# Wide matmuls over both halves of an activation in a first up projection, and a gate's column sum in the down projection

## The reference

```python
mod = c_act @ w_ada[l] + b_ada[l]
sh1, sc1, g1, sh2, sc2, g2 = [m[:, None, :] for m in jnp.split(mod, 6, axis=-1)]
...
h = rmsnorm(x, norm_gains[l, 2]) * (1.0 + sc2) + sh2
y = jnp.square(jax.nn.relu(h @ w1[l] + b1[l])) @ w2[l] + b2[l]
x = x + g2 * rmsnorm(y, norm_gains[l, 3])
```

## Time and profile before

| | us |
|---|---|
| median of three runs | 787.77 |
| the profiled execution | 789.94 |
| its span from first to last instruction | 788.2 |
| PE busy | 734.8 (93% of the span) |
| VectorE busy | 517.8 (66%) |
| ScalarE busy | 450.2 (57%) |
| GpSimd busy | 44.4 (6%) |
| one low half `wl` on VectorE, mean of 217 | 1.23 |

### The profile page before, as it was taken

How to read it: one execution, slowest core, us unless ns; L and a number is a source line. 1 busy time by engine, 2 the same in 40 slices (tenths; PEclk the granted TensorE clock), 3 DMA queues, 4 the chain that set the end, 5 groups by cost and what they waited for, 6 DMA issues and landing times.

```text
span 788.2 us, 12072 instructions
## 1 busy us (share of the span) xinstructions
PE 734.8 (93%) x4062; PEld 619.8 (79%) x4062; DVE 517.8 (66%) x764; ACT 450.2 (57%) x724; POOL 44.4 (6%) x77
## 2 busy tenths in 40 slices
PE   0599999789999999989999999999897999999998
PEld 0498966589999886767989777777686888888886
DVE  6877697777877643457657465665747777777443
ACT  1654678666666433355455687554446777777331
POOL 3100100100000100014101000000000000000000
PEclk9899999979999999998999999999997999999999
DMA  8999985257787655534763564544444666656661
GB/s 315 368 330 338 262 278 167 81 150 206 233 240 263 213 187 166 175 117 115 227 189 114 181 187 131 164 125 138 148 123 134 179 188 175 201 175 197 203 196 57
DMA packets 137167, 150.50 MB, mean 191 GB/s; under 512 B 6164, under 2 KB 111783, under 8 KB 137129
## 3 DMA queue, kind: packets, MB, share of 16 engines
q1 hardware_dynamic: 135278, 145.28, 59.9%
q10 hardware_dynamic: 1852, 4.75, 1.7%
HBM read 148.57 MB, written 1.44 MB: 190 GB/s over the span
## 4 chain that ended last, share of the span: by engine, by line
PE 80%; DVE 10%; issue 4%; ACT 3%; DMA 3%; POOL 1%; SPq 0%; POOLq 0%; DVEq 0%; ACTq 0%
PE acc L1363 13%; PE acc L1364 13%; PE acc L1365 13%; PE acc L1355 11%; PE acc L1342 6%; PE acc L1344 6%; PE acc L1343 6%; PE acc L1356 5%; DVE ada_sum L1038 3%; DMA raw<-in_w_ada 2%; PE aux L1331 2%; DVE wl L960 1%; DMA raw<-in_w_out 1%; PE acc L1595 1%; ACT wh L594 1%
## 5 line engine op out<-in xcount | busy, mean ns | idle before, releaser
L960 DVE TENSOR_TENSOR wl<-raw,wh 128x1024 fp32r<-128x1024 f32 x217 | 266.2, 1232 | 149.5 <-ACT wh L594 148.4
L594 ACT ACTIVATE wh<-raw 128x1024 fp32r<-128x1024 f32 x217 | 227.9, 1055 | 125.6 <-PE acc L1365 109.6
L1342 PE MATMUL acc<-xT,wh 128*128 128x256 f32 x440 | 126.9, 288 | 5.5 <-DVE xT L990 4.1
L1355 PE MATMUL acc<-xT,wh 128*128 128x512 f32 x352 | 127.0, 405 | 0.8 <-DVE xT L982 0.8
L1344 PE MATMUL acc<-xT,wl 128*128 128x256 f32 x440 | 126.1, 287 | 0.0
L1343 PE MATMUL acc<-xT,wh 128*128 128x256 f32 x440 | 126.1, 287 | 0.0
L1363 PE MATMUL acc<-wh,xT 128*128 128x512 f32 (+1 forms) x272 | 111.0, 408 | 4.7 <-DVE xT L982 2.6
L1364 PE MATMUL acc<-wl,xT 128*128 128x512 f32 (+1 forms) x272 | 106.5, 391 | 0.0
L1365 PE MATMUL acc<-wh,xT 128*128 128x512 f32 (+1 forms) x272 | 106.3, 391 | 0.0
L1356 PE MATMUL acc<-xT,wl 128*128 128x256 f32 x352 | 100.0, 284 | 0.0
L1342 PEld LDWEIGHTS acc<-xT,wh 128*128 128x128 f32 x440 | 85.9, 195 | 7.5 <-issue 5.9
(11 more groups left out here) (260 smaller groups left out, 877.1 us busy)
## 6 DMA issues: line engine op xcount, KB each, us to landing
raw<-in_w_in SPq DMA_DIRECT2D x66, 512.0 KB, 3.6
raw<-in_w SPq DMA_DIRECT2D x64, 512.0 KB, 3.8
raw<-in_w_ffn_in SPq DMA_DIRECT2D x44, 512.0 KB, 4.1
raw<-in_w_ada SPq DMA_DIRECT2D x27, 512.0 KB, 6.5
raw<-in_w_ffn_out SPq DMA_DIRECT2D x22, 512.0 KB, 4.3
raw_more<-in_w_ada SPq DMA_DIRECT2D x13, 512.0 KB, 7.2
raw<-in_w_out SPq DMA_DIRECT2D x13, 512.0 KB, 4.8
rows_tmp<-in_w_ada ACTq DMA_DIRECT2D x8, 512.0 KB
```

The lines of the kernel that those rows point to most:

```text
L594: A(wh[:, s, :], raw_unit, ACT.Copy).then_inc(rounded, 1)
L960: V.tensor_tensor(wl[:, s, :], raw_slot(r), wh[:, s, :].bitcast(f32), ALU.subtract).then_inc(split_ready, 1)
L1342: mm(bank[:, 0:ROWS], wh[:, s, w], hi, start=(kt == 0), stop=False)
L1355: mm(bank[:, :], wh[:, s, w], moving[:, kt, :], start=(kt == 0), stop=False, skip_group_check=True)
```

## The change

PE's loop of the up projection calls `both_unit` in place of `col_unit`. ScalarE now copies the second half of the bank with the bias (Identity) into `act_t`, and signals `up1_copied`; DVE adds the first half to it, which frees the bank, and makes max(a, 0) * a, the squared Relu, in `val_t`; ScalarE copies that, rounded, into the high half of `hid`; DVE subtracts as before. The gate's sum leaves the up projection: its first eighth is loaded and added between the two loops, the other seven at the end of the seven iterations of the loop that prepares weights for the down projection.

```diff
@@ ScalarE
-                    A(act_t[:, k, :], acc[k][:, 0:ROWS], ACT.Relu, bias=vT[:, bass.ds(V_B1 + k + RING * i, 1)]).then_inc(acc_free, 1)
-                    act.wait_ge(acc_free, F_PROJ1 + k + 1 + RING * i)
-                    A(hid[:, RING * i + k, 0:ROWS], act_t[:, k, :], ACT.Square).then_inc(hid_hi, 1)
-                    if k == 1:
-                        act.wait_ge(g2_used, i + 1)
-                        act.dma_start(xr[:, 0, :], w_ada_rows[bass.ds(P * i, P), D * C_G2:]).then_inc(g2_full, 16)
+                    A(act_t[:, k, :], acc[k][:, ROWS:], ACT.Identity, bias=vT[:, bass.ds(V_B1 + k + RING * i, 1)]).then_inc(up1_copied, 1)
+                    act.wait_ge(hid_sq, RING * i + k + 1)
+                    A(hid[:, RING * i + k, 0:ROWS], val_t[:, k, :], ACT.Copy).then_inc(hid_hi, 1)
+            act.dma_start(xr[:, 0, :], w_ada_rows[0:P, D * C_G2:]).then_inc(g2_full, 16)
             with act.Fori(0, D_FF // P // RING - 1) as i:
                 for k in range(RING):
                     round_looped(U_DOWN1 + AHEAD, i, k)
+                    if k == RING - 1:
+                        act.wait_ge(g2_used, i + 2)
+                        act.dma_start(xr[:, 0, :], w_ada_rows[bass.ds(P * i + P, P), D * C_G2:]).then_inc(g2_full, 16)
@@ VectorE
                 for k in range(RING):
+                    dve.wait_ge(up1_copied, RING * i + k + 1)
+                    V.tensor_tensor(act_t[:, k, :], acc[k][:, 0:ROWS], act_t[:, k, :], ALU.add).then_inc(acc_free, 1)
+                    dve.wait_ge(acc_free, F_PROJ1 + k + 1 + RING * i)
+                    V.scalar_tensor_tensor(out=val_t[:, k, :], in0=act_t[:, k, :], scalar=0.0, in1=act_t[:, k, :],
+                                           op0=ALU.max, op1=ALU.mult).then_inc(hid_sq, 1)
                     low_unit(U_UP1 + AHEAD + k + 1 + RING * i, slot_of(U_UP1 + AHEAD + k), slot_of(U_UP1 + AHEAD + k))
-                    dve.wait_ge(acc_free, F_PROJ1 + k + 1 + RING * i)
-                    V.tensor_tensor(val_t[:, k, :], act_t[:, k, :], act_t[:, k, :], ALU.mult).then_inc(hid_sq, 1)
                     dve.wait_ge(hid_sq, RING * i + k + 1)
                     dve.wait_ge(hid_hi, RING * i + k + 1)
                     V.tensor_tensor(hid[:, RING * i + k, ROWS:], val_t[:, k, :], hid[:, RING * i + k, 0:ROWS].bitcast(f32),
                                     ALU.subtract).then_inc(hid_ready, 1)
-
-                dve.wait_ge(g2_full, 16 * i + 32)
-                dve.wait_ge(g2_used, i + 1)
-                V.scalar_tensor_tensor(out=G2[:, :], in0=xr[:, 0, :], scalar=cT[:, bass.ds(i, 1)], in1=G2[:, :],
-                                       op0=ALU.mult, op1=ALU.add).then_inc(g2_used, 1)
+            dve.wait_ge(g2_full, 32)
+            dve.wait_ge(g2_used, 1)
+            V.scalar_tensor_tensor(out=G2[:, :], in0=xr[:, 0, :], scalar=cT[:, 0:1], in1=G2[:, :],
+                                   op0=ALU.mult, op1=ALU.add).then_inc(g2_used, 1)
             with dve.Fori(0, D_FF // P // RING - 1) as i:
                 for k in range(RING):
                     low_unit(U_DOWN1 + AHEAD + k + 1 + RING * i, slot_of(U_DOWN1 + AHEAD + k), slot_of(U_DOWN1 + AHEAD + k))
+                dve.wait_ge(g2_full, 16 * i + 48)
+                dve.wait_ge(g2_used, i + 2)
+                V.scalar_tensor_tensor(out=G2[:, :], in0=xr[:, 0, :], scalar=cT[:, bass.ds(i + 1, 1)], in1=G2[:, :],
+                                       op0=ALU.mult, op1=ALU.add).then_inc(g2_used, 1)
@@ TensorE
-                    col_unit(U_UP1 + k, U_UP1 + k + 1 + RING * i, acc[k], xT, columns_ready(X_UP1) if k == 0 else None)
+                    both_unit(U_UP1 + k, U_UP1 + k + 1 + RING * i, acc[k], xT, columns_ready(X_UP1) if k == 0 else None)
```

More of the change, by code:

```diff
@@ L334, in build_program @@
         part_copied, gate_up_done = sem("part_copied"), sem("gate_up_done")
+        up1_copied = sem("up1_copied")
         sig_done, merged_ready = sem("sig_done"), sem("merged_ready")
```

## The result

The changed kernel takes 798.07 us (median of four runs, 793.83 to 798.4) against 787.66 (786.7 to 790.63) of the kernel before in the same series: the medians are 10.4 us apart. The ratio over all the runs is 1.0102 with a 95% interval of 1.0074 to 1.0131, which makes 8 us (6 to 10). The forecast was 796.2, in a range of 791.0 to 800.5. The profiled execution took 798.01, its span is 796.3; before 789.94 and 788.2.

What follows compares the result with a forecast made beforehand. PE's pace was taken to bound the kernel, with loss wherever PE waits for something new. Terms -1.7 + 2.8 + 5.3 + 2.0 = +8.4 us on the 787.8 median gave 796.2 us, range 791.0 to 800.5.

Steps and rivals of the forecast that it cites:

- part 1: First up projection: PE takes 0.353 us per kt instead of 0.36, a gain of 1.7 us.
- part 3: Seam between projections: VectorE waits for the gate's first load, unit 3's low half comes late, PE loses 2.8 us.
- part 4: Seven sums inside the down projection: VectorE's waits cost nothing; the cover is gone with a landing of over 8 us.
- part 5: End of the gate: last load, sum and product have no cover, so PE waits 5.3 us before the spread.
- part 6: Behind the new 5.3 us idle, PE runs at 1.2 GHz for about 4 us, a loss of 2.0 us.
- The 0.6 us that came of the Trainium skill's issue gap: Up projection: alternative estimate of the saving from one matmul fewer per kt, 2.5 ns each over 256; not used.
- Part 2: Up projection: the ScalarE-VectorE exchange takes 11.63 us per four units against PE's 11.30; ScalarE lags 2.6 us at the end.
- rival (a): Up projection: ScalarE keeps up, lag near zero, part 3 costs 0.2; +5.8, 793.6 us; chance 0.25.
- its sign in the waits: Late in the up projection, ScalarE's copy out of the bank shows hardly any wait for PE.
- rival (c): Seam and gate's end: landings slow at 6.4 us, parts 3 and 5 each grow by 2.7; +13.8, 801.6 us; chance 0.10.
- rival (b): Behind the gate's wait: the clock stays at 2.4 GHz; +6.4, 794.2 us; chance 0.12.
- Rival (d): Gate's end: roundings run ahead of PE, last load isn't late, parts 5 and 6 vanish; +1.1, 788.9 us; chance 0.04.

Runs made afterwards that it cites:

- the early kernel: Changed kernel with the gate's first load before the up projection, later loads and sums earlier in each down-projection iteration: 786.89 us, ratio 0.9986.
- the early gate: Gate's loads and sums at those early places: on the changed kernel 786.89 us; on the kernel before, with its old up projection, 789.06 us, ratio 1.0012.

## Why the prediction held, step by step

| term | forecast | in after |
|---|---|---|
| part 1, PE's pace | -1.7 | -1.8 |
| part 3, the seam | +2.8 | +1.8 |
| part 4, sums inside the down projection | 0 | 0 |
| part 5, the last sum uncovered | +5.3 | +7.1 |
| part 6, the clock | +2.0 | +2.9 |
| sum | +8.4 | +10.0 |
| pace of the second up projection | 0 | -2.3 |

**Part 1** was right in after: 0.3533 a `kt` and 1.8 us of gain. That after had the slower of the two paces is chance, as far as is known: against the old loop at the same place (94.24), the early kernel gained 1.9 in the profile at 0.3533 and 3.4 in the one at 0.3467. The 0.6 us that came of the Trainium skill's issue gap ("TensorE: Matmul & The Clock Gate", "Back-to-back issue gap") is too small by a factor of three here. That section gives the formula for a matmul by itself and says that in a stream the loads of the weights count too; here each matmul has its own load of weights (750 of either in the earlier trace rows), which the prediction didn't say.

**Part 2** failed in its result: ScalarE has no lag at the end. The last copy out of the bank starts at 255.76, 0.38 behind the next stage's first matmul, the same 0.38 as in the earlier trace rows. Timeline of after, one unit of the exchange:

```profile
249.26 1.05 ACT L595 ACTIVATE wh<-raw 128x1024 fp32r<-128x1024 f32 x1
...
250.21 0.45 ACT L800 ACTIVATE act_t<-acc,vT 128x256 f32<-128x256 f32 x1
...
250.69 0.42 DVE L1139 TENSOR_TENSOR act_t<-acc,act_t 128x256 f32<-128x256 f32 x1 [0.41 <-ACT act_t L800]
...
251.15 0.43 DVE L1141 SCALAR_TENSOR_TENSOR val_t<-act_t 128x256 f32<-128x256 f32 x1
...
251.70 0.42 ACT L802 ACTIVATE hid<-val_t 128x256 f32 x1 [1.04 <-DVE val_t L1141]
...
252.03 1.05 ACT L595 ACTIVATE wh<-raw 128x1024 fp32r<-128x1024 f32 x1
```

The period is 2.77 us, not 2.86: copy to sum took 0.48 (0.56 taken) and sum to product 0.46 (0.54), product to copy 0.55 (0.47), the rest within 0.02. Four units with the loop's turn take 11.30 (roundings at 235.17 and 246.47), not 11.63. This is rival (a) in its cause (given 0.25), and a near thing: the exchange needs 11.29 by itself, and PE 11.30. What the prediction said of its sign in the waits was half right. ScalarE does wait for PE at the first copy only, and for VectorE at every `hid` copy (waits of after from 166 to 256):

```profile
ACT hid L802 <- DVE val_t L1141: 32.3, 31, 1.0
DVE act_t L1139 <- ACT act_t L800: 16.2, 31, 2.0
ACT act_t L800 <- PE acc L1364: 2.6, 1, 2.6
```

Before there were 25.7 us of waits for PE; that slack has been used up by the exchange. The sign was there without the lag. Where PE ran at 0.3467, in the early kernel's first profile, the exchange was the slower of the two (11.29 against 11.09), and a lag came about as part 2 describes it: PE lost 0.78 us to it at the seam.

**Part 3** had two errors against each other: no lag (2.6 taken), and a landing of 5.27 (3.7 taken). By its own chain, 8.4 without a lag, the longer landing gives 10.0 behind the stage's start, and PE went on at 265.28 - 255.38 = 9.9. So the right chain, at a loss 1.0 below the forecast, came of a lag too much and 1.6 of landing too little. VectorE's program order turned the late load into a late `wl`, as described.

**Part 4** held in after, and gave way in one kernel at a landing of 8.20 us, where its bound had been put at 8.

**Part 5** was right in its mechanism and too small by 1.8, of which 1.7 is the landing: 5.41 instead of 3.7. This landing is the mis-sized term of the prediction. The landings of the earlier trace rows are those of SP's own stream, in one execution, and the prediction took a value near their median for a second stream beside it. In after the eight loads on ScalarE's queue needed from some 4 to 7.5 us from issue to sum, which is the region of rival (c), put at 6.4; its time of 801.6 assumed the lag too. POOL took 2.35, as the earlier trace rows has it without a neighbour. The Trainium skill's rule on the shared ports ("SBUF — State Buffer", "Who interferes with whom") agrees: VectorE was idle there, and the blocked 3.31 did not occur. In the three profiles with the early gate, where VectorE began a `wl` 0.22 us behind the start of this product, the product took 2.40 and that `wl` 3.25 instead of 1.23, ending 1.1 behind the product.

**Part 6** was right in kind, rival (b) was wrong: behind 7.1 us of idle time the granted clock is 0.50. It cost 2.9 and not 2.0, since the low clock lasted beyond the transposes into unit 28.

**The total** in the profile came out at +8.1, beside +8.4, because the misses had both signs: landings +3.3 and clock +0.9 on one side, the missing lag of 2.6 and 2.3 of the pace that differs from one execution to the next on the other (and 0.4 that was there when the up projection began). So that it came so near is in part luck. The medians (798.07 and 787.66) don't hang on that one profile; 798.07 is 1.9 above the forecast, and their difference is 10.4 where 8.4 was forecast. Rival (d), not slower, failed at the point named: ScalarE's rounding of unit 30 waits for PE (1.66 us at 335.94 in after, as in the earlier trace rows). Where the load is tied to an earlier rounding, the loss is gone, and this is what the early kernel did.

## What to carry to other kernels

Work that is moved out of a full stage must end before its reader, not only fit into idle time: measure the chain behind its last piece (here load, sum, product, 9.4 us from issue to PE) and start that piece earlier by this much. A wait on PE can cost more than it lasts: the one of 7.1 us cost 2.8 to 2.9 us by the clock behind it, and one of 1.74 us, in the wide matmuls with the sums left in place, some 1.6; behind the 1.55 us at the seam of after the clock stayed at 1.00. Price a load by landings that were measured beside the other stream and in more than one execution, and give a bound for each lag that is only a difference of two near sums (11.63 and 11.30 here), since either sign of it is open.

## What the runs showed of the hardware

- A pair of matmuls (512 and 256 columns) in the same code runs at a distance of 0.3533 or 0.3467 us, constant within a stage as long as PE doesn't wait, and different from one execution to the next. In the one stage where PE waited again and again, either value stood between the waits. It moves this kernel by 2.3 us in the second up projection and by 1.5 in the first (92.32 and 90.87 in the two early profiles), and it may be a part of the spread between runs of one kernel (785.6 to 791.2 before; its two profiled executions, one of either pace, took 789.94 and 787.94), which only the profiled runs could show. What sets it was not found.
- 512 KB in rows of 4 KB on ScalarE's queue landed in some 3.6 to 8.2 us beside SP's stream. SP's own 32 loads had a median of 3.4 and 4.2 in the two profiles of the kernel before, where the gate's loads ran beside the first few only, and 4.7 in after.
- Idle times of 5.10 us and 7.1 us were both followed by a granted clock of 0.50 (1.2 GHz), and so was one of 1.74 us behind a stage with many short waits (0.51 from 264.40 to 267.80); one of 1.55 us behind a busy stage was not. With other matmuls in the 7.1 us it stayed at 1.00.
- A product of 128x1024 on GpSimd and a `wl` of the same size on VectorE delay each other: the product took 3.31 us where the `wl` began 0.16 ahead of it and 2.40 where it began 0.22 behind, and that `wl` then took 3.25 instead of 1.23.
